# Squares of a norm added in pairs on GpSimd, five products with ones in place of eight

## The reference, cut to what matters

```python
def layer_norm(x, g, b):                      # 4 times
    mu = jnp.mean(xf, axis=-1, keepdims=True)
    xc = xf - mu
    var = jnp.mean(xc * xc, axis=-1, keepdims=True)
    y = xc * lax.rsqrt(var + LN_EPS) * g + b

def rms_norm_2(x, g):                         # 3 times
    y = xf * lax.rsqrt(jnp.mean(xf * xf, axis=-1, keepdims=True) + EPS)
```

## Time and profile before

| | |
|---|---|
| median of 3 runs | 2514.3 us (2513.07 to 2517.81) |
| profiled execution | 2518.29 us, span 2516.5 us |
| TensorE busy | 2377.9 us, 94% |
| VectorE / ScalarE / GpSimd busy | 861.2 / 892.2 / 1207.4 us |
| mean granted TensorE clock | 0.975 |

### The profile page before, as it was taken

The page is one execution under the profiler, slowest core; times in us unless marked ns, Lnnn a source line. Parts: engine busy times, 40 slices in busy tenths (PEclk is TensorE's granted clock), DMA queues, the critical chain, the costliest instruction groups (busy, mean ns, idle before and its releaser), DMA issues.

```text
span 2516.5 us, 31824 instructions
## 1 busy us (share of the span) xinstructions
PE 2377.9 (94%) x12487; PEld 1897.4 (75%) x12487; DVE 861.2 (34%) x1431; ACT 892.2 (35%) x1255; POOL 1207.4 (48%) x1060
## 2 busy tenths in 40 slices
PE   7999999899999889999979999988999989999997
PEld 6777776588888667777758888866888778989896
DVE  3555445411221321656432122132544223313131
ACT  2333433433233433555343322344233224323232
POOL 3455556344444355777634444444312325545452
PEclk8999999999999999999989999998999989999999
DMA  4222221132232122111222322312211112232321
GB/s 126 68 66 69 67 67 64 54 101 92 92 100 89 62 84 76 51 51 51 76 77 84 100 87 97 100 59 83 64 42 35 52 49 68 84 100 83 100 81 53
DMA packets 235323, 188.96 MB, mean 75 GB/s; under 512 B 9216, under 2 KB 226749, under 8 KB 235085
## 3 DMA queue, kind: packets, MB, share of 16 engines
q1 hardware_dynamic: 231504, 183.66, 23.5%
q10 hardware_dynamic: 3708, 3.79, 0.5%
HBM read 185.30 MB, written 2.10 MB: 74 GB/s over the span
## 4 chain that ended last, share of the span: by engine, by line
PE 84%; POOL 7%; ACT 3%; issue 2%; DVE 2%; DMA 1%; SPq 0%; DVEq 0%; ACTq 0%; POOLq 0%
PE ps L2426 47%; PE ps L2518 12%; PE ps L1328 7%; PE ps L615 4%; POOL w_lo L1725 3%; PE ps L2457 1%; PE ps L2617 1%; POOL hdd L403 1%; POOL hdd L401 1%; PE ps L1298 1%; PE ps L1387 1%; ACT w_hi L1880 1%; PE ps L1436 1%; PE ps L681 1%; PE ps L2639 1%
## 5 line engine op out<-in xcount | busy, mean ns | idle before, releaser
L1725 POOL TENSOR_TENSOR w_lo<-raw,w_hi 128x512 fp32r<-128x512 f32 (+2 forms) x760 | 904.1, 1221 | 930.9 <-ACT w_hi L1880 930.2
L1880 ACT ACTIVATE w_hi<-raw 128x2048 fp32r<-128x2048 f32 (+2 forms) x190 | 330.0, 1738 | 527.9 <-PE ps L2426 356.1
L2426 PE MATMUL ps<-a_hi,w_hi 128*128 128x512 f32 (+1 forms) x1232 | 426.3, 369 | 44.1 <-POOL a_lo L1741 20.3
L2426 PE MATMUL ps<-a_hi,w_lo 128*128 128x512 f32 (+1 forms) x1232 | 424.1, 368 | 0.0
L2426 PE MATMUL ps<-a_lo,w_hi 128*128 128x512 f32 (+1 forms) x1232 | 424.0, 368 | 0.0
L2426 PEld LDWEIGHTS ps<-a_hi,w_hi 128*128 128x128 f32 x1232 | 224.8, 191 | 95.9 <-issue 44.8
L2426 PE MATMUL ps<-b_hi,w_hi 128*128 128x512 f32 x720 | 283.4, 394 | 3.0 <-DVE hv L1272 3.0
L2426 PE MATMUL ps<-b_hi,w_lo 128*128 128x512 f32 x720 | 284.8, 396 | 0.0
L2426 PE MATMUL ps<-b_lo,w_hi 128*128 128x512 f32 x720 | 283.2, 393 | 0.0
L2426 PEld LDWEIGHTS ps<-a_lo,w_hi 128*128 128x128 f32 x1232 | 223.7, 192 | 39.5
L2426 PEld LDWEIGHTS ps<-a_hi,w_lo 128*128 128x128 f32 x1232 | 224.6, 192 | 38.2
(11 more groups left out here) (332 smaller groups left out, 3794.8 us busy)
## 6 DMA issues: line engine op xcount, KB each, us to landing
raw<-in_mlp_w_dram SPq DMA_DIRECT2D x128, 512.0 KB, 4.3
raw<-in_w_up_dram SPq DMA_DIRECT2D x44, 512.0 KB, 5.0
raw<-in_ssd_w_in_dram SPq DMA_DIRECT2D x40, 512.0 KB, 4.8
raw<-in_hgrn_w_in_dram SPq DMA_DIRECT2D x48, 256.0 KB, 3.2
raw<-in_w_in_dram SPq DMA_DIRECT2D x24, 512.0 KB, 4.8
raw<-in_ssd_w_out_dram SPq DMA_DIRECT2D x16, 512.0 KB, 4.3
raw<-in_ple_w_gate_dram SPq DMA_DIRECT2D x16, 512.0 KB, 4.5
raw<-in_w_down_dram SPq DMA_DIRECT2D x16, 512.0 KB, 4.0
```

Of the source, the lines that this page charges most:

```text
L1725: last = nc.gpsimd.tensor_tensor(w_lo[:, slot, piece], raw[:, slot, i * q:(i + 1) * q], w_hi[:, slot, piece].bitcast(F32), ALU.subtract)
L1880: nc.scalar.activation(w_hi[:, slot, at:at + n], raw[:, slot, 0:n], ACT.Copy).then_inc(whi_ready, 1)
L2426: last = nc.tensor.matmul(ps[:, b + s, 0:nn], w[:, k, m * P:(m + 1) * P], v[:, k, c0 + s * nn:c0 + (s + 1) * nn], start=(k == 0 and first) ...
```

## The change

In each of the seven norms GpSimd adds squares 0 and 1, 2 and 3, and 4 and 5 in place, into the slot of the first. TensorE multiplies five tiles with ones: the sums of the pairs (called product 0, 2 and 4 here) and squares 6 and 7, in the order 0, 2, 6, 4, 7. Squares 4 and 5 on ScalarE wait for product 0, squares 6 and 7 for product 2. GpSimd's adds stand in its queue right before the low parts of the norm, and for norm 6 at the end. The order of sums in fp32 changes, nothing else in what is computed. `sq_at` now counts norms and no longer products.

```diff
+SQ_ORDER = (0, 2, 6, 4, 7)
+SQ_FREE = (0, 0, 0, 0, 1, 1, 2, 2)
...
+        def add_pairs(pool, norm, n):
+
+            for j in range(3):
+                pool.wait_ge(ln_sq, KD * norm + 2 * j + 2)
+                a, b = 2 * j % 4, (2 * j + 1) % 4
+                nc.gpsimd.tensor_tensor(sq[:, a, 0:n], sq[:, a, 0:n], sq[:, b, 0:n], ALU.add).then_inc(sq_pair, 1)
+
         def block2_pool(pool, chunk, pub, b_at, cut_lo):
-            def publish2_lo():
+            def publish2_lo(norm):
+                add_pairs(pool, norm, L2)
                 for k in range(KD):
...
             with turns(pool, 2, {chunk: 12, b_at: 8}):
                 ffn(8, False)
             ffn(6, True)
+            add_pairs(pool, 6, L2)
...
                 for k in range(KD):
                     act.wait_ge(there, before + k + 1)
-                    act.wait_ge(sq_used, sq_at(k - 3 if k >= 4 else 0))
+                    act.wait_ge(sq_used, 5 * sq_at.n + SQ_FREE[k])
                     nc.scalar.activation(sq[:, k % 4, :], res[:, k, :], ACT.Square).then_inc(ln_sq, 1)
-                sq_at.add(KD)
-                act.wait_ge(sq_used, sq_at())
+                sq_at.add()
+                act.wait_ge(sq_used, 5 * sq_at.n)
...
             def rms2_pe():
-                for k in range(KD):
-                    pe.wait_ge(ln_sq, sq_at(1))
+                for k in SQ_ORDER:
+                    if k < 6:
+                        pe.wait_ge(sq_pair, 3 * sq_at.n + k // 2 + 1)
+                    else:
+                        pe.wait_ge(ln_sq, KD * sq_at.n + k + 1)
                     for s in range(2):
                         last = nc.tensor.matmul(bank[4 + s][:, 0:H2], ones, sq[:, k % 4, s * H2:(s + 1) * H2],
                                                 start=(k == 0), stop=(k == KD - 1))
                     last.then_inc(sq_used, 1)
-                    sq_at.add()
+                sq_at.add()
...
             def ln_lo(i):
+                add_pairs(pool, i, T)
                 for k in range(LN_LO):
```

More of the change, by code:

```diff
@@ L345, in two_blocks @@
                                                         sem("sq_used"), sem("rstd_ready"))
+        sq_pair = sem("sq_pair")
         pcol_done, pcol_ready = sem("pcol_done"), sem("pcol_ready")
@@ L821, in publish2_lo @@
                     pub.add()
-            publish2_lo()
+            publish2_lo(4)
             cut_lo(1)
@@ L853, in block2_pool @@
             cut_lo(0)
-            publish2_lo()
+            publish2_lo(5)
             def ffn(nt, last):
```

## The result

The median of 16 runs is 2519.87 us (2517.33 to 2526.10), beside 2514.76 us for the kernel before (16 runs, 2512.73 to 2517.81). The ratio is 1.0023, 95% interval 1.0015 to 1.0030: slower by 5.1 us. The forecast was 2512.5 with a range up to 2518.5. The profiled execution took 2525.41 us, the second longest of the 16, with a span of 2523.6 us.

A forecast was written before the change was run, and what follows sets the result against it. The products with ones, and their clock, were taken to bound each norm. Norms 0 to 4 gave +0.7 us and norms 5 and 6 -2.8, together -2.1; applied to the 2514.3 median, 2512.2, stated as 2512.5, range 2507.5 to 2518.5.

The forecast's parts named there:

- What bounds a norm: In a norm the products with ones are the bound, 0.86 us each at full clock, 1.71 us at half clock.
- The handover from GpSimd to TensorE: Time from the end of a GpSimd add to the TensorE product that uses it, taken as 0.18 us.
- Norms 5 and 6: Adds hidden behind TensorE's other products; Ln at 5.9 us in place of 7.33, 2.8 us saved in both.
- The full-clock schedule: Norms 0 to 4 with TensorE at 2.4 GHz: product 0 starts at 2.73 us, Ln at 8.7 after the first square.
- +0.84 us: Norm 0 at full clock: Ln 0.84 us later than the 7.86 us before, despite three products fewer.
- The step that failed: Norms 0 to 4: longer TensorE idle time, 3.6 us, puts product 0 and all or part of product 2 at half clock.
- the term 9.8 us per norm: First square to Ln in norms 0 to 4: 9.8 us used, 9.75 in norms 1 and 3, 9.9 in norm 4.
- The term for norms 0 to 4: Differences of +1.9, +0.2, -0.7, +0.2 and -0.9 us in first square to Ln, together +0.7 us.
- The rival of half clock throughout: All five products in norms 0 to 4 at 1.2 GHz, Ln at 11.6 us; +7.0 us in total, 2521.3; chance 0.16.
- Its argument against itself: At half clock an add's 1.25 us is less than a product's 1.71, so products 0 and 2 lie close together.
- GpSimd has nothing else to do at the norms: GpSimd is idle in norms 0 to 4 while the adds would run; its low halves come later than every add.
- nothing outside the norms moves: Only Ln ends late in a norm, everything after it moves by the same amount, and the rest costs nothing.

The follow-up runs named there:

- Only the head filled: The changed kernel with products whose results are overwritten put only ahead of product 0, none between products 2 and 6: 2507.40 us against 2516.15 for the kernel before.

## Why the prediction was wrong

- **What bounds a norm** was read rightly: the products, and the clock they run at. The start of product 0 (2.7 us forecast, 2.55 to 2.64), GpSimd's adds (1.25 us forecast, 2.50 for two in norm 0; 1.28 forecast for 528 columns, 1.30 to 1.34), and that the adds hide in norm 5 are as forecast. The handover from GpSimd to TensorE was put too high: 0.04 us, not 0.18.
- **Norms 5 and 6**: -2.8 us forecast, -2.89 in the profile, -2.9 (-0.5 to -5.0) with the pairs in these two alone.
- **The full-clock schedule** of norms 0 to 4 is right to 0.1 us wherever the clock was 1.00. Where the prediction explains its +0.84 us by 2.04 and 0.99 against 2.6, it leaves out the 0.39 us between products 0 and 2 that its own schedule has; the +0.84 is right.
- **The step that failed** is "I take product 0 at half clock in every one of norms 0 to 4, and product 2 wholly or partly", and so the term 9.8 us per norm. In norms 0, 1, 3 and 4 the half clock lasted until the last product or into it, and Ln came at 11.9 to 12.2 us; only norm 2 came to 10.0. The term for norms 0 to 4 was +0.7 us; it measured +9.9 in the profile and +10.2 (6.5 to 13.6) with the pairs there alone. I took the return of the clock after two or three products from the earlier trace rows, where the eight products run without a hole. In the changed kernel they don't. The rival of half clock throughout had this mechanism and a difference of +7.0 us; the profile has +7.1. It was given 0.16. That it comes so close is partly luck: four norms came 0.3 to 0.6 us later than its 11.6 us and one 1.6 us earlier, and 2.1 and 1.3 us less elsewhere happen to balance the 3.6 more between norms 4 and 5. Its argument against itself, that products 0 and 2 lie close together, was true and did not matter: the hole behind product 2 is enough.
- **The reason**, as shown: idle time ahead of product 0 goes with the half clock. With fillers there, and ahead of the mean's product, the clock stays at 1.00. The hole between products 2 and 6, where it falls into the half clock, delays the return: with the hole filled the clock returns within 6.0 us, and eight products in a row get it back within 5.2 us after the same idle time. The longer idle time alone is not the loss: 1.55 and 2.15 us were enough for the half clock in norms 1 to 3 before the change, and eight products started as late lost 1.4 to 2.6 us per norm to it, where the five products with the hole lost 3.3 to 3.6 in four norms (the windows less 7.17 and 6.0 us; 7.4 and 6.2 in norm 4). In norm 2 the clock was back before the hole came, in this profile and in that of pairs in norms 0 to 4. There it had fallen earlier, 3.3 us before product 0 against 1.2 to 1.9 in norms 0, 1 and 3; but in norm 4 it fell 5.1 us before and still came back late, so why it is norm 2 both times stays open.
- **The median** moved by 5.1 us (3.8 to 7.5 by the interval), less than the profile's 7.1. The parts measured by themselves, +10.2 and -2.9, give 7.3, which lies within the noise of all three. An earlier return of the clock in the unprofiled runs is not the reason: averaged over the run it was 0.971 to 0.973 in all sixteen, 0.971 in the profiled one.
- That GpSimd has nothing else to do at the norms held: no add waited for other work, and x minus mean still took 4.87 to 4.88 us. That nothing outside the norms moves came true as a sum, less than 0.1 us, but by parts of up to 3.6 us that cancel.
- The low clock of norms 0 to 4 before the change was itself worth 10.2 us by the medians (8.8 in the profiles), three and a half times what the pairs gain in norms 5 and 6; the prediction saw it and treated it as given.

## What to carry to other kernels

Work taken off TensorE counts only if TensorE then goes on at the same clock: where a change makes it start later and leaves holes between what remains, price what remains at 1.2 GHz to the end as one of the cases, and read the granted clock in windows of the size of the step, not the mean. Before removing products from a short serial stage, try filling its idle time with products that nobody reads: here that gave 10 us for five norms. Removing three of eight products gave 3 us, and only in the two norms where other products ran directly ahead; with the clock held by fillers it cost 3.7 us in the other five.

## What the runs showed of the hardware

A hole of 0.78 us at full clock left the granted clock at 1.00 in five norms ("Only the head filled"). Where the same hole fell into the half clock, the clock was back only 8.3 to 9.0 us after product 0, against 5.1 to 6.0 with a product in the hole. The same pattern of products ran 6.0 us in the one case and, in four norms of five of the changed kernel, 9.3 to 9.7 us in the other.

A VectorE instruction with both inputs in SBUF on 8 partitions stood 4.61 us beside four GpSimd subtractions in a row that had started 0.98 us earlier; begun 0.90 us after the first of them in the kernel before, it took 0.94 us, and the four lasted 1.4 us longer.
